# The triangular inverse of the chunked recurrence on compact 32x32 diagonal blocks

## The reference, cut to what matters

```
def step(S, inp):                      # S: 64x64 per head, 16 heads, 2 directions
    S = S * w_t - (S @ kk_t) outer (kk_t * a_t) + v_t outer k_t
    y = S @ r_t
```

## Time and profile before

| | |
|---|---|
| median of 3 runs | 2382.64 us (2382.05 to 2384.68) |
| span of the profiled execution | 2385.3 us |
| PE busy | 2263.7 us, 95% of the span |
| DVE busy | 1452.8 us, 61% |
| ACT busy | 1005.5 us, 42% |
| the five levels and all else of one context chunk | 43.7 us |

### The profile page before, as it was taken

One profiled execution on the slowest core, in us unless ns is written; L12 is line 12 of the kernel. 1 busy time (PEld: TensorE's weight loads), 2 busy tenths in 40 slices (PEclk: granted clock), 3 DMA queues, 4 the chain that ended last, 5 costly groups with the idle time before them and its releaser, 6 DMA issues.

```text
span 2385.3 us, 46871 instructions
## 1 busy us (share of the span) xinstructions
PE 2263.7 (95%) x20728; PEld 1862.9 (78%) x20728; DVE 1452.8 (61%) x2443; ACT 1005.5 (42%) x1768; POOL 48.3 (2%) x53
## 2 busy tenths in 40 slices
PE   8999999999999999999999999998999999899997
PEld 5864478888867788899988899896677879667786
DVE  3273436867746357887774553465475876656576
ACT  2243333332313224544432464344354655444564
POOL 1000000000000000000000000020000002000000
PEclk9999999999999999999999999998999999999999
DMA  8235237756522100000002356544355863204484
GB/s 350 106 124 195 88 129 296 262 196 247 213 79 106 36 1 4 3 4 3 12 3 101 133 177 243 217 159 177 142 184 216 332 221 142 71 1 177 174 338 176
DMA packets 47307, 348.03 MB, mean 146 GB/s; under 512 B 5264, under 2 KB 5280, under 8 KB 5760
## 3 DMA queue, kind: packets, MB, share of 16 engines
q1 hardware_dynamic: 45936, 334.52, 37.6%
q0 software_dynamic: 1168, 10.51, 1.1%
HBM read 343.96 MB, written 1.05 MB: 145 GB/s over the span
## 4 chain that ended last, share of the span: by engine, by line
PE 79%; DVE 12%; ACT 6%; issue 1%; DMA 1%; DVEq 0%; ACTq 0%
PE banks L544 27%; PE banks L2210 7%; PE banks L1009 6%; PE banks L3077 3%; PE banks L3078 3%; PE banks L3079 3%; PE banks L2069 2%; PE banks L1827 2%; PE banks L609 2%; PE banks L855 2%; PE banks L3108 2%; PE banks L2287 2%; PE banks L3110 2%; PE banks L3109 2%; PE banks L556 1%
## 5 line engine op out<-in xcount | busy, mean ns | idle before, releaser
L522 DVE TENSOR_TENSOR mlp_w_low<-weight_slots,mlp_w_high 128x2048 fp32r<-128x2048 f32 x64 | 146.5, 2289 | 194.9 <-ACT mlp_w_high L513 194.9
L522 DVE TENSOR_TENSOR moe_w_low<-weight_slots,moe_w_high 128x2048 fp32r<-128x2048 f32 x96 | 217.9, 2289 | 61.9 <-ACT moe_w_high L513 61.2
L513 ACT ACTIVATE mlp_w_high<-weight_slots 128x2048 fp32r<-128x2048 f32 x64 | 122.2, 1910 | 182.7 <-PE banks L544 118.2
L513 ACT ACTIVATE moe_w_high<-weight_slots 128x2048 fp32r<-128x2048 f32 x96 | 181.7, 1914 | 23.8 <-PE banks L3110 19.7
L2210 PE MATMUL banks<-weight_slots,arena 64*64 64x64 f32 (+1 forms) x3648 | 147.3, 223 | 18.9 <-ACT arena L2230 13.3
L2210 PEld LDWEIGHTS banks<-weight_slots,arena 64*64 64x64 f32 x3648 | 139.1, 134 | 27.3 <-ACT arena L2230 15.2
L1009 PE MATMUL banks<-arena,weight_slots 128*128 128x256 f32 (+1 forms) x512 | 145.6, 440 | 3.0 <-DVE arena L2744 1.5
L1009 PEld LDWEIGHTS banks<-arena,weight_slots 128*128 128x128 f32 x512 | 99.0, 194 | 44.2 <-issue 33.6
L3077 PE MATMUL banks<-moe_w_high,slots_x 128*128 128x512 f32 x320 | 129.6, 405 | 2.8 <-DVE moe_w_low L522 2.8
L3078 PE MATMUL banks<-moe_w_low,slots_x 128*128 128x512 f32 x320 | 126.4, 395 | 0.0
L3079 PE MATMUL banks<-moe_w_high,slots_x 128*128 128x512 f32 x320 | 126.3, 395 | 0.0
(11 more groups left out here) (444 smaller groups left out, 5038.0 us busy)
## 6 DMA issues: line engine op xcount, KB each, us to landing
weight_slots<-weights SPq DMA_DIRECT2D x318, 1024.0 KB, 4.9
arena<-small POOLq DMA_DIRECT2D x1, 2560.0 KB, 9.1
arena<-x_t POOLq DMA_DIRECT2D x1, 2048.0 KB, 11.1
arena<-bias POOLq DMA_DIRECT2D x1, 2048.0 KB, 10.7
constants<-consts POOLq DMA_DIRECT2D x1, 1410.0 KB, 17.5
out_t<-arena SPq DMA_DIRECT2D x1, 1024.0 KB, 3.9
parameters<-params POOLq DMA_DIRECT2D x1, 763.0 KB, 21.3
arena<-pool_inv POOLq DMA_DIRECT2D x1, 512.0 KB, 14.5
```

The lines of the kernel that those rows point to most:

```text
L513: nc.scalar.activation(self.pair(j)[0], slot(j, 0, SLOT), ACT.Copy).then_inc(*act.step("high", j))
L522: nc.vector.tensor_tensor(self.pair(j)[1], slot(j, 0, SLOT), self.pair(j)[0], ALU.subtract).then_inc(*v.step("used", j))
```

## The change

Levels 1 to 4 never leave the 32x32 blocks on the diagonal. They now work on these alone: a tile for one direction is 128 partitions (four strips of 32: two heads, two diagonal blocks each) by 8x32 = 256 columns, and the group of products is 32 matmuls of 32x32 by 32, each strip q from partitions 32q to the PSUM partitions 32q. Level 5 joins the two diagonal blocks of a head: z is one 32x32 product per head, written to the other strip, Z is a copy without a mask, and grow one 32x32 product per head back; the inverse is then assembled by ACT in a 64-wide tile (`inverse_out` writes the new quadrant, `inverse_half` the diagonal ones, with the others set to zero by a scale per partition). `first_inverse` folds the 64-wide masked tile to 32 columns with one more addition.

```diff
+        def blocks_matmul(pe, out, strips, lhs, rhs, opens):
+            opened = set()
+            for p in range(PAIRS):
+                for q, to in strips:
+                    ins = nc.tensor.matmul(out[strip(to), p * 32:p * 32 + 32], lhs(p, q), rhs(p, q),
+                                           start=opens == "all" or (opens == "first" and to not in opened), stop=True,
+                                           skip_group_check=True)
+                    opened.add(to)
+            return ins
+
+        SAME_STRIPS = [(q, q) for q in range(4)]
+        OWN_TO_OTHER = [[(0, 1), (2, 3)], [(1, 0), (3, 2)]]
+        OTHER_TO_OWN = [[(1, 0), (3, 2)], [(0, 1), (2, 3)]]
...
+            def level(c, d, lv):
+                b = take_bank(pe, ("z", c, d, lv), WORK_BANKS)
+                X_, BM = WK["X"][:, d], bm_of(c, d)
...
+                if lv < LEVELS - 1:
+                    strips, column = SAME_STRIPS, lambda q: 32 * (q % 2)
+                else:
+                    strips, column = OWN_TO_OTHER[d], lambda q: 32 * (1 - q % 2)
+                ins = blocks_matmul(pe, psum(b, 0, 256), strips, lambda p, q: BM[strip(q), p, column(q):column(q) + 32],
+                                    lambda p, q: X_[strip(q), p, :], "all")
...
             def grow(c, d, lv):
...
-                for p in range(PAIRS):
-                    for h in range(2):
-                        r = half(h)
-                        ins = nc.tensor.matmul(psum(b, p * 64, 64, r), Z[r, p, :], XI[r, p, :], start=False,
-                                               stop=True, skip_group_check=True)
+                last = lv == LEVELS - 1
+                ins = blocks_matmul(pe, psum(b, 0, 256), OTHER_TO_OWN[d] if last else SAME_STRIPS,
+                                    lambda p, q: Z[strip(q), p, :], lambda p, q: XI[strip(q), p, :],
+                                    "first" if last else "none")
...
                 for lv in range(1, LEVELS):
                     for d in range(2):
-                        X_, BM = WK["X"][:, d], bm_of(c, d)
-                        pairs_matmul(pe, ("z", c, d, lv), lambda p, r: [(BM[r, p, 0:64], X_[r, p, :])],
-                                     ready=[("bm_out", c, d), ("inverse", c, d, lv - 1)])
+                        level(c, d, lv)
...
             def inverse_out(c, d, lv):
-                nc.scalar.activation(flat(XI_OF[c % 2][:, d]), psum(INVERSE_BANKS[d]), ACT.Copy).then_inc(
-                    *act.step("inverse_t", c, d, lv))
+                src = psum(INVERSE_BANKS[d], 0, 256)
+                if lv < LEVELS - 1:
+                    nc.scalar.activation(flat(WK["XI"][:, d]), src, ACT.Copy).then_inc(*act.step("inverse_t", c, d, lv))
+                else:
+                    nc.scalar.activation(WK["INVERSE"][:, d, :, 32 * (1 - d):32 * (1 - d) + 32],
+                                         src.rearrange("p (a b) -> p a b", b=32), ACT.Copy).then_inc(
+                        *act.step("inverse_t", c, d, lv))
+
+            def inverse_half(c, d):
+                act.wait_ge(*act.own)
+                nc.scalar.activation(WK["INVERSE"][:, d, :, 32 * d:32 * d + 32], WK["XI"][:, d], ACT.Copy,
+                                     scale=cn("own_rows", d, 1)).then_inc(*act.step("inverse_half", c, d))
...
-                tt(XI, bm[:, :, 0:64], first, mul).then_inc(*v.step())
+                tt(FIRST, bm[:, :, 0:64], first, mul).then_inc(*v.step())
+                if c:
+                    v.wait_ge(*after("inverse_half", c - 1, d))
+                v.wait_ge(*v.own)
+                tt(XI, FIRST[:, :, 0:32], FIRST[:, :, 32:64], add).then_inc(*v.step())
                 v.wait_ge(*v.own)
                 tt(XI, XI, I, add).then_inc(*v.step("inverse_t", c, d, 0))
...
-                nc.vector.transpose(flat(WK["X"][:, d]), psum(INVERSE_BANKS[d])).then_inc(*v.step("inverse", c, d, lv))
+                nc.vector.transpose(flat(WK["X"][:, d]), psum(INVERSE_BANKS[d], 0, 256)).then_inc(
+                    *v.step("inverse", c, d, lv))
...
-                        tt(WK["Z"][:, d], bank3(("z", c, d, lv)), mask, mul).then_inc(*v.step("taken", "z", c, d, lv))
+                        src = psum(bank_of(("z", c, d, lv)), 0, 256).rearrange("p (a b) -> p a b", b=32)
+                        if lv < LEVELS - 1:
+                            mask = cn("block_levels", (d * 4 + lv - 1) * 32, 32).unsqueeze(1).to_broadcast([P, PAIRS, 32])
+                            ins = tt(WK["Z"][:, d], src, mask, mul)
+                        else:
+                            ins = nc.vector.tensor_copy(WK["Z"][:, d], src)
```

More of the change, by code:

```diff
@@ L79, in constants @@
     c["first_level"] = np.concatenate([first(r, s), first(s, r)], 1)
-    later = []
+    r32, s32 = (i % 32)[:, None], np.arange(32)[None, :]
+    levels = []
     for direction in range(2):
[L82 to L85, removed]
+        for lv in range(1, LEVELS - 1):
+            a, b = (r32 >> lv, s32 >> lv) if direction == 0 else (s32 >> lv, r32 >> lv)
+            levels.append((a // 2 == b // 2) & (a % 2 == 1) & (b % 2 == 0))
+    c["block_levels"] = np.concatenate(levels, 1)
     c["ident64"] = (r == s)
+    c["ident32"] = (r32 == s32)
+    c["own_rows"] = np.stack([i // 32 % 2 == 0, i // 32 % 2 == 1], 1)
     c["scan_keep"] = np.broadcast_to(np.arange(512) % CHUNK != 0, (P, 512))
@@ L2212, in pairs_matmul, with strip @@
             ins.then_inc(*pe.step(*key))
+        def strip(q):
+            return slice(32 * q, 32 * q + 32)
+        def blocks_matmul(pe, out, strips, lhs, rhs, opens):
[10 more added lines that the diff above has]
+        OTHER_TO_OWN = [[(1, 0), (3, 2)], [(0, 1), (2, 3)]]
         def pairs_turned(pe, key, src, ready=()):
@@ L2273, in seed @@
                 pe.wait_ge(*after("inverse_t", c, d, 0))
-                nc.tensor.matmul(psum(b), cn("ident"), flat(XI_OF[c % 2][:, d]), start=True, stop=True).then_inc(
+                nc.tensor.matmul(psum(b, 0, 256), cn("ident"), flat(WK["XI"][:, d]), start=True, stop=True).then_inc(
                     *pe.step("seed", c, d))
+            def level(c, d, lv):
+                b = take_bank(pe, ("z", c, d, lv), WORK_BANKS)
+                X_, BM = WK["X"][:, d], bm_of(c, d)
+                pe.wait_ge(*after("bm_out", c, d))
+                pe.wait_ge(*after("inverse", c, d, lv - 1))
+                if lv < LEVELS - 1:
[4 more added lines that the diff above has]
+                                    lambda p, q: X_[strip(q), p, :], "all")
+                ins.then_inc(*pe.step("z", c, d, lv))
             def grow(c, d, lv):
-                b, XI, Z = INVERSE_BANKS[d], XI_OF[c % 2][:, d], WK["Z"][:, d]
+                b, XI, Z = INVERSE_BANKS[d], WK["XI"][:, d], WK["Z"][:, d]
                 pe.wait_ge(*after("z_out", c, d, lv))
@@ L2424, in seeded @@
                 act.wait_ge(*after("inverse_t", c - 1, d, LEVELS - 1))
-                nc.scalar.activation(psum(INVERSE_BANKS[d]), flat(XI_OF[c % 2][:, d]), ACT.Copy).then_inc(
+                nc.scalar.activation(psum(INVERSE_BANKS[d], 0, 256), flat(WK["XI"][:, d]), ACT.Copy).then_inc(
                     *act.step("seeded", c, d))
@@ L2459, in wkv_scalar @@
                     if lv in (1, 4):
-                        system_out("w", "U", c, 0 if lv == 1 else 1)
+                        system_out("w", "W", c, 0 if lv == 1 else 1)
+                    if lv == LEVELS - 2:
+                        for d in range(2):
+                            inverse_half(c, d)
                     if lv == 1 and not ahead:
@@ L2651, in wkv_vector @@
                     for d in range(2):
[L2652 removed]
                         v.wait_ge(*after("z", c, d, lv))
[L2654 removed]
+                        src = psum(bank_of(("z", c, d, lv)), 0, 256).rearrange("p (a b) -> p a b", b=32)
[4 more added lines that the diff above has]
+                            ins = nc.vector.tensor_copy(WK["Z"][:, d], src)
+                        ins.then_inc(*v.step("taken", "z", c, d, lv))
                         v.mark("z_out", c, d, lv)
```

28 lines of the change are left out of this document (14 added, 14 removed).

## The result

| | before | after |
|---|---|---|
| median | 2383.7 us (2382.1 to 2388.2) | 2431.3 us (2428.3 to 2433.8) |
| ratio | | 1.0201 [1.0189, 1.0214] |
| span of the profiled execution | 2385.3 us | 2430.6 us |
| granted clock, mean over the span | 0.980 | 0.959 |

The account below looks back on a forecast made before the run. The prediction took PE to bound the kernel up to level 2's masks, then the chain through DVE and ACT; gains of 34.0, 5.2 and 7.8 us made 47, from 2382.6 to 2336 us, own range 2328 to 2347, 8-in-10 range 2325 to 2410.

Parts of the forecast that it names:

- the chain through DVE and ACT: In a context chunk's levels, gains beyond level 2's masks must pass through DVE and ACT; level 5's grow starts 4.85 us earlier.
- the part set at 16: Halved DVE and ACT work in the levels, with PE's group time unchanged: 2.3 us a chunk, 16 us over seven chunks.
- the sum: Levels of chunks 0 to 6 34.0 us, level 5's grow 5.2, chunk 7 7.8: together 47 us less.
- The cost of a group in the array: Levels 1 to 4: 64 records as 16 rounds of 32 ns, four strips at once, 0.52 us; level 5's group also 0.52.
- the 58.4 ns of a round: Two 64-column quadrant records per round; 115 ns at twice the columns, so taken to follow column count, about 32 at 32 columns.
- I take 0.52: Choice for a group of 64 records in levels 1 to 4, between ends of 0.52 and 1.87 us.
- Rival 1: Every z and grow of levels 1 to 4: issue bound near 29.2 ns a record, 2476 us, slower; chance 0.23.
- The break-even: Levels 1 to 4: PE turns to a loss above about 1.1 us a group, 17 ns a record.
- the 2440 us: Levels 1 to 4 by the skill's rule of about 25 ns between matmul starts: 1.6 us a group, some 2440 us.

Follow-up runs that it names:

- narrow_reads: Kernel before, with masks, transposes and ACT's copies of the levels on 256 of 512 columns, the other half left out: 2362.14 us, ratio 0.9910.
- half_pairs: Changed kernel with half the products of z and grow in levels 1 to 4 left out: 2342.16 us beside 2383.29, ratio 0.9838.
- level5_only: Kernel before with level 5 alone changed (one 32x32 product per head for z and grow, narrow copy): 2385.70 us beside 2383.29, ratio 1.0013.
- block_stationary: Changed kernel's narrow tiles with before's call count, 16 calls of 64x64 stationary by 32 moving columns: 2369.50 us beside 2384.02, ratio 0.9935.
- bursts: Kernel before plus three bursts of 256 four-strip calls ahead of level 1, with 32, 64 and 128 moving columns: 2425.62 us beside 2384.02.
- wide_moving: Changed kernel with z and grow of levels 1 to 4 moving 64 columns instead of 32, same calls: 2415.98 us, ratio 1.0132.

## Why the prediction was wrong

*What bounds it, the chain through DVE and ACT.* Right in the main. narrow_reads gives 21 us for the part set at 16. half_pairs, with the instructions of before, lands at 2342, inside the forecast's own range of 2328 to 2347, but with half of the products missing, so it supports the chain and does not confirm the sum.

*The cost of a group in the array.* Nearly right inside a page: four strips do run at once, and 128 records in 1.27 us are 0.64 us a group for the predicted 0.52. Level 5's group has its 0.52 (two in 1.04 us, level5_only). Against that, the argument that the 58.4 ns of a round follow the moving columns does not hold for the 64x64 block: with 32 columns it takes as long as with 64 (block_stationary).

*"What no row shows is the rate at which PE can issue such short records for long … I take 0.52."* This step failed. In bursts a page of 128 records lasts 3.46 to 3.73 us, so a group of 64 costs about 1.8 us whenever groups follow one another. The upper end had been written down, 1.87, and the lower was taken because rows 9 showed four strips at once. Those rows held 16 records. In bursts 174 run before the first stop, so a row that short could not tell a burst from a pace. Nor could rows 8, whose 57.4 ns a record are slower than the supply. And before's 29.2 ns a record are 3.74 us for 128, the pace of the pages itself; whether that or the weight load of the 64x64 block set them, no run separates.

*Rival 1* had place and sign, and its pace of 29.2 ns a record is the one found. Its mechanism was another: not each record is slow to issue, but instructions arrive in pages. What it expected of the profile, PE fully busy in the levels, did not show either: PE is busy for 27.26 of 37.97 us and waits for the rest. Its 2476 us was 45 too high; pages that arrive while PE waits for others would explain that, which no run tested by itself. By pages: a context chunk had 1152 records, 9 pages, and has 512 more now, 13 pages, which at 3.7 us need 48 us of the chunk's 49.2 to 52.8. Before, 9 pages lay in 43.7 us, 4.9 each, hidden. The break-even, 17 ns a record, was passed.

The rule of the Trainium skill in "TensorE: Matmul & The Clock Gate", section "Wait — 56ns, not 53.3ns?", of some 25 ns between starts, doesn't hold within a page here, where records start 10 ns apart. The pace over many pages, 27 to 29 ns, is close to it, and the 2440 us worked out by it was the nearest figure in the prediction, in part by luck, since it charges each record what is a matter of whole pages. The Trainium skill's "Runtime: NRT & Kernel Launch", section "Instruction fetch mechanics", names the blocks of 256 instructions and says that crossing into the next is mostly hidden. This case's trace agrees on the 256 and not on the hiding.

*The clock* was in no term and no rival. The account: forecast -47 (half_pairs -41 with the lost products), measured +48. The second half of the calls costs 89 us; at least 15 of these come back with a higher clock (wide_moving, as I read it), the rest is supply and the array's own work. How the rest divides wasn't measured.

## What to carry to other kernels

Before a product is split into smaller tiles, count PE's instructions: a float32 call is two LDWEIGHTS and two MATMULs, and 128 such pairs were supplied every 3.46 to 3.73 us in steady bursts. Tiles of 64x64 by 64, at 29.2 ns a pair, sit on that pace, so here smaller products in more calls lost, and only the forms that kept the number of calls gained. Narrowing the moving columns and keeping the blocks, as block_stationary does, made no group of PE in levels 1 to 4 faster, but it kept the calls and halved the work of DVE and ACT. Look at the granted clock behind each new wait. And before a row is taken for a pace, count its records: 16 of them cannot show what 128 are supplied at.

## What was not expected of the hardware

- Instructions for PE in pages of 256, one per 3.46 to 3.73 us in steady bursts, at a granted clock of 0.50 as at 1.00; the profile names the stop "issue", with no releaser.
- A wait of 1.65 us on PE among narrow groups was followed by bm at a granted clock of 0.61, 2.96 us for 64 records of 1.87; three products without use in that wait kept the clock at 1.00 and were worth 12 us of the kernel.
- A transpose of 128x256 on DVE took 0.445 us for 0.703 at twice the width.
- 64 records of a 64x64 block took 2.0 us with 32 moving columns as with 64.
